# Odd mixer of a diffusion transformer: the loop over head pairs unrolled, its steps reordered, two heads alternating

## The reference, cut to what matters

```python
def odd_mixer(h, hc, w_in, w_out, rel_bias, ctx_out):
    rows = S // GRID_W
    kh = min(NA_ROWS_MAX, rows)
    q, k, v = jnp.split(h @ w_in, 3, axis=-1)
    kc, vc = jnp.split(hc @ w_in[:, C_WIDTH:], 2, axis=-1)
    ...
    def row_block(r):
        ...
        s_loc = jnp.einsum('bhqd,bhiqjd->bhqij', qr, kw).astype(jnp.float32) * C_SCALE + bias.astype(jnp.float32)
        s_ctx = jnp.einsum('bhqd,bhkd->bhqk', qr, kc_h).astype(jnp.float32) * C_SCALE
        s = jnp.concatenate([s_loc.reshape(B, C_HEADS, GRID_W, n_loc), s_ctx], axis=-1)
        p = jax.nn.softmax(s, axis=-1).astype(vw.dtype)
        ...
        return (jnp.einsum('bhqij,bhiqjd->bhqd', p_loc, vw)
                + jnp.einsum('bhqk,bhkd->bhqd', p[..., n_loc:], vc_h))
    ...
    y = o.transpose(1, 0, 3, 2, 4).reshape(B, S, C_WIDTH) @ w_out
```

## Time and profile before

| | |
|---|---|
| median of 3 executions | 3282.23 us (3281.8 to 3283.03) |
| the profiled execution | 3282.25 us |
| its span, first to last instruction | 3280.5 us |
| TensorE matmul busy | 2987.8 us, 91% |
| VectorE busy | 1182.9 us, 36% |
| ScalarE busy | 716.3 us, 22% |
| granted TensorE clock, mean | 0.954 |
| odd mixer, first score product to output product | 2425.4 to 2681.5 us |

### The profile page before, as it was taken

How to read it: one execution, slowest core, us unless ns; L and a number is a source line. 1 busy time by engine, 2 the same in 40 slices (tenths; PEclk the granted TensorE clock), 3 DMA queues, 4 the chain that set the end, 5 groups by cost and what they waited for, 6 DMA issues and landing times. The chain is left out here.

```text
span 3280.5 us, 36518 instructions
## 1 busy us (share of the span) xinstructions
PE 2987.8 (91%) x13278; PEld 1698.2 (52%) x13278; DVE 1182.9 (36%) x2763; ACT 716.3 (22%) x1392; POOL 3.0 (0%) x8
## 2 busy tenths in 40 slices
PE   6999799999999979989898999999978777999997
PEld 3545344444577667874545444444445555444443
DVE  2421687720356647602322232232333223222222
ACT  1332200000455520002411111111122222222121
POOL 0000000000000000000000000000000000000000
PEclk9989899999999989999898999999999988999999
DMA  5132555522212037640024888888522116999995
GB/s 234 66 123 92 198 228 230 230 102 109 84 65 66 25 127 298 267 154 25 12 114 167 336 333 325 336 337 319 230 71 70 58 58 275 399 396 397 397 393 214
DMA packets 98651, 652.76 MB, mean 199 GB/s; under 512 B 10256, under 2 KB 18704, under 8 KB 21904
## 3 DMA queue, kind: packets, MB, share of 16 engines
q1 hardware_dynamic: 98576, 651.74, 51.2%
HBM read 650.65 MB, written 1.05 MB: 199 GB/s over the span
## 5 line engine op out<-in xcount | busy, mean ns | idle before, releaser
L577 PE MATMUL PB<-A,RING 128*128 128x512 f32 (+1 forms) x1408 | 463.0, 492 | 29.2 <-DVE BIG L630 11.6
L577 PEld LDWEIGHTS PB<-A,RING 128*128 128x128 f32 x1408 | 271.5, 193 | 220.8 <-issue 183.7
L610 DVE SCALAR_TENSOR_TENSOR WORK<-RING,MORE 128x1024 f32<-128x1024 f32 x288 | 335.5, 1221 | 19.0 <-ACT MORE L591 10.6
L2060 PE MATMUL PB<-RING,BIG 128*64 128x512 f32 x1536 | 340.6, 592 | 0.0
L418 PE MATMUL PB<-BIG,RING 128*128 (+2 forms) x928 | 310.7, 497 | 5.6 <-PEq L545 3.3
L2242 DVE TENSOR_TENSOR BIG<-BIG,PB 64x512 f32<-64x512 f32 x64 | 44.1, 690 | 710.3 <-ACT BIG L2141 710.3
L2092 PE MATMUL PB<-BIG 128*128 128x512 f32 (+1 forms) x544 | 211.8, 512 | 46.2 <-DVE X L2249 42.4
L418 PEld LDWEIGHTS PB<-BIG,RING 128*128 128x128 f32 x928 | 175.9, 190 | 139.3 <-issue 128.7
L2060 PEld LDWEIGHTS PB<-RING,BIG 128*64 128x64 f32 x1536 | 110.2, 137 | 218.3 <-issue 218.1
L2046 PE MATMUL PB<-WORK,BIG 128*128 128x128 f32 x1632 | 197.2, 279 | 5.1 <-DVE WORK L2236 5.1
L2046 PEld LDWEIGHTS PB<-WORK,BIG 128*128 128x128 f32 x1632 | 191.5, 195 | 5.3 <-issue 5.3
(11 more groups left out here) (345 smaller groups left out, 3222.2 us busy)
## 6 DMA issues: line engine op xcount, KB each, us to landing
RING<-moe_w SPq DMA_DIRECT2D x288, 1024.0 KB, 7.4
MORE<-moe_w SPq DMA_DIRECT2D x96, 1024.0 KB, 7.9
RING<-ada_rows SPq DMA_DIRECT2D x72, 1024.0 KB, 6.8
RING<-ffn_w SPq DMA_DIRECT2D x66, 1024.0 KB, 4.8
RING<-ada_w SPq DMA_DIRECT2D x17, 1024.0 KB, 6.3
RING<-hg_w_in SPq DMA_DIRECT2D x16, 1024.0 KB, 4.9
RING<-odd_w_in SPq DMA_DIRECT2D x8, 1024.0 KB, 5.1
BIG<-ada_w SPq DMA_DIRECT2D x5, 1024.0 KB, 12.7
```

The lines of the kernel that those rows point to most:

```text
L577: last = pe_.matmul(PB[:, 2 * s + j, 0:t], tile(s, KD, P, j * KD * P)[:, k, :], A[:, k, 0:t], start=k == 0, stop=k == KD - 1)
L610: last = dve_.scalar_tensor_tensor(out=JUNK[:, n % 4, :], in0=RING[:, s, b * D:(b + 1) * D], scalar=1.0, in1=WIDE[:, side // 2, w, :], op0 ...
L2060: last = pe_.matmul(PB[m * CAP:(m + 1) * CAP, 0, :], XGT[:, b, k, slots_of(e % 2)], spot_tile(s, 4, T)[:, k % 4, :], start=k == 0, stop=k ...
```

## The change

The loops over m are written out on TensorE, ScalarE and VectorE (SP keeps its loop). On TensorE the order for one pair becomes: scores; queries and keys of the next pair; transposes of both heads; the first half of the next pair's values; the value products of both heads; the second half of the next pair's values. In the scores and the value products the two heads alternate. Both heads' results go to bank 7, one half of the partitions each, and are carried out by one copy. The helpers of `pe_scores`, `pe_apply` and so on are written in place, with one copy of 1024 columns for the transposes of a head, one maximum over both query tiles, and mask additions for both heads ahead of the scores. `staged` is signalled after the keys; the values have a signal of their own. In SP's loop the wait for `biased` and the bias DMA stand first.

```diff
             def _(sp):
                 join.sp(sp)
                 sp.dma_start(BI[:, :, 0:S], bias[0]).then_inc(sig("bias_in").sem, 16)
                 with sp.Fori(1, KD) as m:
+                    sp.wait_ge(sig("biased").sem, sig("biased").at(2 * m))
+                    sp.dma_start(BI[:, :, 0:S], bias[m]).then_inc(sig("bias_in").sem, 16)
                     sp.wait_ge(used[0].sem, used[0].at(m))
                     sp.dma_start(RING[:, 0, :], w_in[m, :, 0:2 * D]).then_inc(loaded[0].sem, 16)
                     sp.wait_ge(used[1].sem, used[1].at(m))
                     sp.dma_start(RING[:, 1, 0:D], w_in[m, :, 2 * D:3 * D]).then_inc(loaded[1].sem, 16)
-                    sp.wait_ge(sig("biased").sem, sig("biased").at(2 * m))
-                    sp.dma_start(BI[:, :, 0:S], bias[m]).then_inc(sig("bias_in").sem, 16)
                 first_rows(sp, io["odd_w_out_2"], KD)
...
+                def project_values(m, w):
+                    if w == 0:
+                        pe.wait_ge(loaded[1].sem, loaded[1].at(16 * (m + 1)))
+                        pe.wait_ge(sig("value_copied").sem, sig("value_copied").at(m))
+                    for t in (2 * w, 2 * w + 1):
                         for k in range(KD):
...
-                def attend(m, more):
+                def scores(m):
                     pe.wait_ge(sig("staged").sem, sig("staged").at(m + 1))
-                    pe.wait_ge(sig("carried").sem, sig("carried").at(2 * m))
+                    for t in range(2):
+                        for i in range(2):
+                            last = pe_.matmul(PB[:, 2 * i + t, :], QB[rows[i], t * P:(t + 1) * P], KB[rows[i]],
+                                              start=True, stop=True)
+                            if t:
+                                last.then_inc(sig("scored").sem, 1)
...
+                def flips(m):
                     for i in range(2):
+                        pe.wait_ge(sig("shared").sem, sig("shared").at(2 * m + i + 1))
+                        for kt in range(NT):
+                            for t in range(2):
+                                last = pe_.transpose(turned_place(i, kt)[:, t * P:(t + 1) * P],
+                                                     PRB[i][:, t, kt * P:(kt + 1) * P], IDENT)
+                        last.then_inc(sig("flipped").sem, 1)
+
+                def weigh(m):
+                    pe.wait_ge(sig("value_copied").sem, sig("value_copied").at(m + 1))
+                    pe.wait_ge(sig("carried").sem, sig("carried").at(m))
+                    pe.wait_ge(sig("turned").sem, sig("turned").at(2 * m + 2))
+                    for kt in range(NT):
+                        for i in range(2):
+                            last = pe_.matmul(PB[rows[i], 7, 0:S], VB[:, kt, rows[i]], PTB[i][:, kt, 0:S],
+                                              start=kt == 0, stop=kt == NT - 1)
+                    last.then_inc(sig("weighted").sem, 1)
...
+                for m in range(KD):
+                    more = m + 1 < KD
+                    scores(m)
                     if more:
+                        project_queries_keys(m + 1)
+                    flips(m)
+                    if more:
+                        project_values(m + 1, 0)
+                    weigh(m)
+                    if more:
+                        project_values(m + 1, 1)
 
             @block.scalar
...
+                for m in range(KD):
                     for i in range(2):
+                        act.wait_ge(sig("peaked").sem, sig("peaked").at(2 * m + i + 1))
...
                     for i in range(2):
+                        act.wait_ge(sig("flipped").sem, sig("flipped").at(2 * m + i + 1))
+                        act_.activation(PTB[i][:, :, 0:S], PB[:, 2 * i:2 * i + 2, :].rearrange("p a (b n) -> p (a b) n", b=2),
+                                        ACT.Copy).then_inc(sig("turned").sem, 1)
+                    if m + 1 < KD:
+                        stage(m + 1)
+                    act.wait_ge(sig("weighted").sem, sig("weighted").at(m + 1))
+                    act_.activation(OT[:, m, 0:S], PB[:, 7, 0:S], ACT.Copy).then_inc(sig("carried").sem, 1)
+                    if m + 1 < KD:
+                        value(m + 1)
 
             @block.vector
...
+                    chain(last)
+                    for i in range(2):
+                        n = 2 * m + i
                         dve.wait_ge(sig("scored").sem, sig("scored").at(n + 1))
...
                         last.then_inc(sig("biased").sem, 1)
                         dve.wait_ge(sig("biased").sem, sig("biased").at(n + 1))
-                        dve_peaks(dve, chain, n, 2, 1.0, biased, i)
+                        dve_.tensor_reduce(HEAD_PEAK[:, i, 0:2], SC[:, 2 * i:2 * i + 2, :], AX.X, ALU.max, negate=True) \
+                            .then_inc(sig("peaked").sem, 1)
```

More of the change, by code:

```diff
@@ L654, in first_key @@
         return 0 if t < 2 else S
[L658 to L714, removed]
@@ L1369, in odd_mixer @@
         QB, KB, VB, SC, BI = own(0, 1, S), own(S, 1), own(S + T, NT, P), own(S + 2 * T, 4), own(S + 6 * T, 4)
+        PRB, PTB = ([w[:, i * 2 * T:(i + 1) * 2 * T].rearrange("p (a n) -> p a n", a=a) for i in range(2)]
+                    for w, a in ((WORK, 2), (MORE, NT)))
+        HEAD_PEAK, HEAD_SHARE = (SMALL[:, 64 * i:64 * i + 8].rearrange("p (b j) -> p b j", b=2) for i in range(2))
         w_in = io["odd_w_in_2"]
@@ L1373, in odd_mixer, with turned_place @@
         near = con("near")
-        def biased(t, b):
-            return SC[:, 2 * b + t, :]
-        each = 4
+        rows = [slice(i * HD, (i + 1) * HD) for i in range(2)]
+        def turned_place(i, kt):
+            return PB[:, 2 * i + kt // 2, (kt % 2) * S:(kt % 2 + 1) * S]
         with nc.Block() as block:
@@ L1394, in _, with project_queries_keys @@
             def _(pe):
-                def project(m, first):
+                def project_queries_keys(m):
                     pe.wait_ge(loaded[0].sem, loaded[0].at(16 * (m + 1)))
                     for k in range(KD):
-                        if first:
+                        if m == 0:
                             join.ready(pe, k)
@@ L1410, in project @@
                                               tile(1, KD, P)[:, k, :], start=k == 0, stop=k == KD - 1)
-                    last.then_inc(used[1].sem, 1)
-                def attend(m, more):
+                    if w:
+                        last.then_inc(used[1].sem, 1)
+                def scores(m):
                     pe.wait_ge(sig("staged").sem, sig("staged").at(m + 1))
-                    pe.wait_ge(sig("carried").sem, sig("carried").at(2 * m))
-                    for i in range(2):
-                        r = slice(i * HD, (i + 1) * HD)
-                        pe_scores(pe, 2 * m + i, 2, [(QB[r], KB[r])], i)
-                    if more:
[L1420 to L1423, removed]
@@ new lines, in _ @@
+                join.pe(pe)
+                project_queries_keys(0)
+                for w in range(2):
+                    project_values(0, w)
+                for m in range(KD):
+                    more = m + 1 < KD
+                    scores(m)
+                    if more:
+                        project_queries_keys(m + 1)
[5 more added lines that the diff above has]
+                        project_values(m + 1, 1)
@@ L1431, in _, with stage, value @@
             @block.scalar
             def _(act):
-                join.act(act)
-                with act.Fori(0, KD) as m:
+                def stage(m):
                     act.wait_ge(used[0].sem, used[0].at(m + 1))
                     act_.activation(QB, PB[:, 4, 0:S], ACT.Copy)
-                    act_.activation(KB, PB[:, 5, :], ACT.Copy)
+                    act_.activation(KB, PB[:, 5, :], ACT.Copy).then_inc(sig("staged").sem, 1)
+                def value(m):
                     act.wait_ge(used[1].sem, used[1].at(m + 1))
@@ L1439, in _ @@
                     act_.activation(VB.rearrange("p a b -> p (a b)"), PB[:, 6, :], ACT.Copy) \
[L1440 to L1446 removed]
+                        .then_inc(sig("value_copied").sem, 1)
@@ new lines, in _ @@
+                join.act(act)
+                stage(0)
+                value(0)
+                for m in range(KD):
+                    for i in range(2):
+                        act.wait_ge(sig("peaked").sem, sig("peaked").at(2 * m + i + 1))
+                        for t in range(2):
+                            last = act_.activation(PRB[i][:, t, :], SC[:, 2 * i + t, :], ACT.Exp, bias=HEAD_PEAK[:, i, t:t + 1],
+                                                   accum_out=HEAD_SHARE[:, i, t:t + 1])
+                        last.then_inc(sig("exped").sem, 1)
+                    for i in range(2):
+                        act.wait_ge(sig("flipped").sem, sig("flipped").at(2 * m + i + 1))
[7 more added lines that the diff above has]
+                        value(m + 1)
@@ L1450, in _ @@
```

(21 more changed lines are left out.)

15 lines of the change are left out of this document (removed).

## The result

The changed kernel takes 3299.48 us (median of four, 3298.61 to 3299.84) against 3282.15 (3281.8 to 3283.03): ratio 1.0052, 95% interval 1.0037 to 1.0067. It is 17.3 us slower; forecast was 22.

What follows compares the result with a forecast made beforehand. TensorE's own order of work, with its holes, was taken to set the pace. Seven pairs +29.0, first scores -0.8, tail -6.8, output product +1 make +22.4 on 3282.25: 3304 us, range 3289 to 3316.

Steps and rivals of the forecast that it cites:

- The hole: TensorE before the next queries and keys: weights issued at 7.04 land at 13.3, wanted at 1.92; new hole 11.4 us.
- The rival in which all three loads mix: SP's loads: bias and both weight loads share the engines, landing at 14.3, 38.6 a pair, 3316 us; 12%.
- The clock: TensorE behind the new hole: half clock after work returns loses 2.6 us a pair, making a pair 37.3.
- The bounds, 1.95 and 2.85: Low and high loss per pair at half clock, from 3.9 and 5.7 us of low clock after two other holes.
- The rival of an unmoved clock: TensorE's clock does not fall in the new hole: pairs at 34.7, time 3284 us; 5%.
- The other, 9 us after each restart: TensorE's clock stays low longer after each hole: 1.9 us more a pair, 3318 us; 6%.
- The pair: TensorE from scores to scores: 23.3 us if weights are in time, 34.7 at full clock with the hole, 37.3 with clock loss.
- Value products: TensorE's value products, alternating between heads in different column halves: both heads take 1.94 us, saving 1.94 a pair.
- 3.9 in single file: Rival for TensorE's value products: heads not concurrent, 1.94 us more in each of eight pairs, 3320 us; 3%.
- Scores: TensorE's alternating score products: heads already run abreast at 1.99 us, so zero gain; strict order would save 1.1 a pair.
- The ends: Before the first scores -0.8 us; from eighth scores to output product 17.3 instead of 24.06, -6.8.
- the forecast's +1: Output product after the mixer may start at half clock: 0 to 2 us, taken as +1.

Runs made afterwards that it cites:

- experiment 1: Changed kernel with SP's loop in the old order, both weight loads ahead of the wait for `biased` and the bias DMA: 3206.07 us, ratio 0.9767.
- experiment 2: Kernel before with only SP's loop changed to the new order, wait for `biased` and bias DMA first: 3374.03 us, ratio 1.0282.
- experiment 7: Changed kernel with two bias buffers, SP's new order kept, so the bias DMA waits only for the pair before the last: 3208.11 us, 0.9774.
- experiment 3: Changed kernel with twelve idle products of 512 columns before the wait for the query/key weights: 3281.26 us, ratio to before 0.9998.
- experiment 6: Kernel of experiment 1 with the score products of head 0 before those of head 1: 3208.83 us, 0.9778.
- experiment 5: Kernel of experiment 1 with all value products of head 0 before those of head 1: 3213.31 us, 0.9791.
- experiment 9: Kernel of experiment 1 with value products alternating in runs of two products a head: 3206.09 us.
- experiment 10: Kernel of experiment 1 with value products in runs of three products a head, then one and one: 3209.35 us.
- experiment 4: Kernel before with ScalarE's loop alone written out: 3261.07 us, ratio 0.9936.

## Why the prediction was right

**The hole.** The step that decided was to follow SP's queue: the wait moved ahead of the loads ends only after the scores, and the loads are wanted right behind these. Experiments 1, 2 and 7 show it from three sides. One reading of the old queue was too short: not only the bias DMA stands behind the wait for `biased`, but also the weights of the next turn. It did not hold them, because their own wait, for `used`, ended later (2438.04 against 2432.68). The size of the hole was taken a little too long. The bias DMA came at 6.26 (6.37 forecast, one reduction of 1.22 us instead of two) and the weight load at 7.08 (7.04), but it landed 5.6 after its issue, not 6.3: half a microsecond more than alone (5.1), although 512 KB were ahead. The sum had the megabyte take 3.2 us from the landing of the bias; it took 2.5 (7.08 + 5.6 against 6.26 + 3.9). What shortened it was not tested. The projection began at 12.6 to 13.1, on average 12.8, instead of 13.3. The rival in which all three loads mix (7.3) did not happen.

**The clock.** 2.6 a pair was forecast from two holes elsewhere; experiment 3 gives 2.57. The bounds, 1.95 and 2.85, came from these holes, but 2.6 was a choice between them, so that it lies this close is luck. From pair to pair the query rows lost 1.5 to 3.0. The rival of an unmoved clock is refuted by the granted 0.82 to 0.86. The other, 9 us after each restart, did not happen either: the key rows behind the queries take 7.03, as at full clock.

**The pair.** Without the hole 23.3 was worked out and 23.40 measured: transposes, copies, staging and value products all fit under one another as written. A pair with the hole was 36.77 on average (37.3 forecast), and 7 x 0.53 = 3.7 is most of the 6.1 by which the sum was above the +16.3 of the spans.

**Value products.** 1.94 for both heads: 1.95. What I set against it, 3.9 in single file, was too much: without alternation, but in one group, it is 2.86. Of the gain over the kernel before (two separate products of 1.94) 1.0 comes from the grouping and 0.91 from the alternation.

**Scores.** Nothing forecast, nothing found: 1.99 at full clock before and after, and in either order at experiment 6. The Trainium skill (TensorE: Matmul & The Clock Gate, The mechanism) says matmuls are never reordered. Experiments 5, 6, 9 and 10 disagree, within the depth that they show: 2.86 us for two runs of eight records, where that rule would give 15 slots, an estimated 3.5.

**The ends.** The first scores began 1.97 earlier instead of 0.8, of which 1.12 was there when the first queries began (2403.26, before 2404.38), ahead of anything the change touches; among the experiments the first scores began between 2422.6 and 2425.7, so this is scatter, and the other 0.85 is the forecast's. Behind the eighth scores 17.3 was forecast, 15.93 measured: the transposes ran at the lower clock (3.67), but the value products no longer did (1.95, not 3.7). In experiment 1 they did (3.68), and its end is 17.67, so the step was right and this size hangs on when the clock comes back. The output product and what follows took 1.11 more, which looks like the forecast's +1 but is not: it was to start at half clock, and it starts at 1.00. This part of the span is 598.4 to 600.1 us in the kernels here, so 1.11 is within their scatter, and the agreement is luck.

**Table load.** I left open whether it would go. It went, and experiment 4 shows it was worth 1.38 a pair where it lay in a hole; in the changed kernel it would have been covered. The forecast rightly did not need it, but it was the cheapest gain to be had in the kernel before: one line for 21 us.

## What to carry to other kernels

When a wait moves in a DMA queue, ask of every load behind it when it is now issued and when it is wanted: here two lines of SP turned a gain of 76 us into a loss of 17. An order of work that fills every hole on the bounding engine also leaves loads less time to land: in experiment 1 the weights issued at 2435.26 are wanted at 2447.91, 12.7 us later instead of 20.6. So the queue must be looked at after the engines' new order, not with the old one. A hole can cost more than its length, by the lower clock behind it: 2.57 us a pair here, and nothing behind the first hole of 3.31 us, where the clock stayed at 1.00; and a loop's head may hold a table load on the critical path that the written-out form does not have.

## What the runs showed of the hardware

TensorE runs products of two row halves, or of two column halves, side by side even when those of the one half are written first, up to four records (two products) deep: eight score records in 1.99 us in either order, and value products in 2.00, 2.43 and 2.86 us with runs of four, six and eight records a head. Depths beyond four were tried with column halves only. A megabyte load issued 0.8 us behind 512 KB landed in 5.6 us against 5.1 alone, and 512 KB behind both in 6.3 against 3.5. Twelve products in the hole kept the clock at 1.00 and were worth 2.57 us a pair, without changing when the work could start.
